# Second half of the output projection: the heads' rests of tiles 1 to 3 placed ahead of tile 1's main products, and tile 2 summed in a bank of its own

## The chip, the core and the metric

The kernel runs on one core of one Trainium2 chip. The metric is the time of one execution on the device in microseconds. Before the change it is 1380.24 us, the median of three runs (1379.95 to 1380.58).

## What is computed

Two decoder layers over 512 tokens of width 1024. Each layer mixes the tokens (layer 0 by a gated convolution, layer 1 by an mLSTM), attends with four heads to a memory of 256 tokens, projects the heads' outputs to width 1024 and adds the layer's input; a layer norm follows, then a mixture of 32 experts, of which a router picks two for each token, and another layer norm.

```python
for i in range(DEPTH):                                    # DEPTH = 2
    h_loc, q_mem = conv_mixer(...) if i % 2 == 0 else mlstm_mixer(...)
    h_mem = cross_attention(q_mem, mem, w_kv_mem[i])
    y = jnp.concatenate([h_loc, h_mem], axis=-1) @ w_out[i]       # 512 x 1024 x 1024
    x = layer_norm(ALPHA * x + y, ln1_g[i], ln1_b[i])
    m = grouped_moe(x, router_w, router_b, w_gate[i], w_up[i], w_down[i])
    x = layer_norm(ALPHA * x + m, ln2_g[i], ln2_b[i])

# in grouped_moe: scores = sigmoid(x2 @ router_w); the best group of 4 experts by the sum of
# its two best; the two best experts in it; gates = their scores, divided by their sum;
# then for each expert: (silu(x @ w_gate[e]) * (x @ w_up[e])) @ w_down[e], times the gate
```

The change touches the line with `w_out` and what is interleaved with it: the sum, the first layer norm and the router.

## The kernel before

**The projection.** The tokens are four tiles of 128 (`TT` = 4), the inner dimension eight slices of 128 (`KT` = 8), the outer dimension two halves of 512 columns. Precision is kept by splitting each operand into a high part and a rest (`hi`, `lo`), so that a slice of a tile takes three products: hi x hi, heads' rest x hi ("the rests"), and hi x weights' rest. The first half of all four tiles is computed slice by slice in banks 0 to 3. The second half follows tile by tile: tile 0 whole (`second(0, ...)`), tile 1 whole (`second(1, ...)`), and for tiles 2 and 3 first the eight products with the heads' rests (`rests(t)`) and later the sixteen others (`mains(t, ...)`: with `w_hi` and `w_lo`). Tile t's second half is summed in `second_bank(t)`, which is bank 4, 5, 4, 3 for tiles 0 to 3; tile 2 therefore waits in `rests(2)` until VectorE has read tile 0's sum out of bank 4 (`summed`).

**What is woven in.** TensorE executes in the order in which `out_pe` is written. Between the products stand, for each tile: `turn(t, b)`, four transposes of half b of the summed rows (for b = 1 they wait for VectorE's sum, `summed`); `route_strips(t)` and `route_sum(t)` (tile 3: `route(3, b)`), the router's logits; `count(t)`, which counts how many earlier tokens picked each expert and waits for VectorE's choice (`chosen`); and `pick_first(t, h)`, which gathers the rows of the first two experts by products.

**VectorE** (`out_dve`) goes tile after tile: `finish_sum(t)` (waits for `b_done`, tile t's last product; adds to the residual at L991, then statistics), `place(t - 1)` (waits for `counted`, L1048 to L1051), `shift`, `invert`, `scale` (layer norm, L1002 to L1010; the last makes `normed`), `scale_logits(t)` (waits for the logits, L1018), `choose(t)` (waits for ScalarE's sigmoid, L1030 to L1042). ScalarE copies the transposes and the strips out of the banks and takes square roots and sigmoids, with a table load between the two.

**The weight stream.** The experts' weights come in units of 2 MB (96 in each layer), in a ring of ten places, all on SyncE's queue and in its order. During the projection the places still hold the projection's own operands, so `out_sp` waits: units 4 and 5 for the first half's end, unit 6 for `rests_read` 1 (the heads' rests are read for the last time, in `rests(3)`), unit 7 for `rests_read` 2 (the weights' rest is read for the last time, in `mains(3, ..., (w_lo,))`), units 8 and 9 for all of the projection (`b_done` 4). Between them SyncE sends each finished tile's rows to memory, after `normed`. From unit 10 on, a load waits until TensorE has read what was in its place; the first three of these units come in pieces, each as soon as a part of the place is free (`part_read`).

```python
second_bank = lambda t: bank[3] if t == TT - 1 else bank[4 + t % 2]
# out_sp
for t in range(TT - 1):
    if t:
        sp.wait_ge(rests_read, t)
        load_unit(sp, l, 5 + t)
    sp.wait_ge(normed, t + 1)
    sp.dma_start(x1_dram[l]..., x_sb[:, t, :]).then_inc(stored, 16)
sp.wait_ge(b_done, TT)
```

The experts themselves (`gate_up`, L1313, and `down`, L1358) run in the order of the stream after it. The whole happens twice, in layer 0 (projection at about 140 to 203 us) and in layer 1 (862 to 921 us).

Of the kernel before, what the change touches and what calls it, by code (L numbers as in the profile page):

```python
# [34 lines left out]
TT = SEQ // P  # L35
KT = D_MODEL // P
# [37 lines left out]
def build_trunk(nc, x, xT_in, memT_in, conv_slabs, conv_qm, mlstm_w_in, smalls, w_kv_mem, w_out,  # L74
                ln1_g, ln1_b, ln2_g, ln2_b, w_pack, out):
    ctx = ExitStack()
    with ctx:
# [56 lines left out]
        bank = [ctx.enter_context(nc.psum_tensor(f"bank{i}", [P, 512], F32)) for i in range(8)]  # L134
# [555 lines left out]
        def out_blocks(l, ph, mem_l, pad, ln_rows, conv, xgT0, ln2_rows, xturned, xcopied, stored, indexed):  # L690
# [20 lines left out]
            in_ln, a_done, b_done, half_summed, summed = s("in_ln"), s("a"), s("b"), s("half_summed"), s("summed")  # L711
# [6 lines left out]
            CODES, PICKED, POS_AT = 2 + PER_GROUP, N_EXPERTS + N_GROUPS, 256  # L718
            w_raw, w_half = w_out_raw, w_out_half
            h_half = heads_half[l]  # L720
            second_bank = lambda t: bank[3] if t == TT - 1 else bank[4 + t % 2]
            logits_of = lambda t: bank[t % 2][:, 0:N_EXPERTS]
            strips_of = lambda t: bank[t % 2][:, P:2 * P]
            pos_of = lambda t: bank[t % 2][:, POS_AT:POS_AT + PICKED]
# [41 lines left out]
            def out_pe(pe):  # L766
                first_ks = range(KT if conv else 6)

                def project(o, n, t, k, first=False):
                    (w_hi, w_lo), (h_hi, h_lo) = ((a[:, k, :] for a in w_half[n]), (a[:, k, t * P:(t + 1) * P] for a in h_half))  # L770
                    for i, (a, b) in enumerate(((h_hi, w_hi), (h_lo, w_hi), (h_hi, w_lo))):
                        if first and i == 0:
                            continue
                        last = nc.tensor.matmul(o[:, :], a, b, start=(k == 0 and i == 0), stop=(k == (KT if n else len(first_ks)) - 1 and i == 2))
                    return last

                def rests(t):
                    if t == 2:
                        pe.wait_ge(summed, 1)
                    else:  # L780
                        pe.wait_ge(half_summed, t + 1)
                    for k in range(KT):
                        last = nc.tensor.matmul(second_bank(t)[:, :], h_half[1][:, k, t * P:(t + 1) * P], w_half[1][0][:, k, :],
                                                start=(k == 0), stop=False)
                    if t == TT - 1:
                        last.then_inc(rests_read, 1)

                def mains(t, ks, parts):
                    for k in ks:
                        for w in parts:  # L790
                            last = nc.tensor.matmul(second_bank(t)[:, :], h_half[0][:, k, t * P:(t + 1) * P], w[:, k, :],
                                                    start=False, stop=(k == KT - 1 and w is parts[-1] and w_half[1][0] in parts))
                    if ks[-1] == KT - 1:
                        last.then_inc(b_done if w_half[1][0] in parts else rests_read, 1)

                def second(t, ks):
                    for k in ks:
                        if t == 0:
                            pe.wait_ge(lo_ready, n_first + k + 1)
                        last = project(second_bank(t), 1, t, k)  # L800
                    if ks[-1] == KT - 1:
                        last.then_inc(b_done, 1)

                def turn(t, b):
                    if b == 0:
                        pe.wait_ge(half_summed, t + 1)
                    else:
                        pe.wait_ge(summed, t + 1)
                    if t == 0 and b == 0:
                        pe.wait_ge(gw_ready, 2)  # L810
                    if t:
                        pe.wait_ge(copied, 2 * t - 1 + b)
                    for j in range(4):
                        k = 4 * b + j
                        last = nc.tensor.transpose(T_BANK[b][:, j * P:(j + 1) * P], x_sb[:, t, k * P:(k + 1) * P], ident[:, :])
                    last.then_inc(turned, 1)

                def may_route(t, b):
                    pe.wait_ge(copied, 2 * t + b + 1)
                    if b == 0 and t < 2:  # L820
                        pe.wait_ge(half_summed, t + 1)
                    elif b == 0:
                        pe.wait_ge(first_marked, 2 * t - 2)

                def route_strips(t):

                    for b in range(2):
                        may_route(t, b)
                        for j in range(4):
                            last = nc.tensor.matmul(strips_of(t)[32 * j:32 * j + 32, :], gw[:, 0, 4 * b + j, :],  # L830
                                                    turned_x[t % 2][:, 4 * b + j, :], start=(b == 0), stop=(b == 1))
                    last.then_inc(routed, 1)

                def route_sum(t):

                    pe.wait_ge(strips_out, t + 1)
                    nc.tensor.matmul(logits_of(t), strips[:, :], strip_sum[:, :], start=True, stop=True).then_inc(routed, 1)
# [9 lines left out]
                def count(t):  # L847

                    pe.wait_ge(chosen, t + 1)
                    for q in range(t + 1):  # L850
                        last = nc.tensor.matmul(pos_of(t), before[:, :] if q == t else ones_bf[:, :],
                                                taken[:, q, :], start=(q == 0), stop=(q == t))
                    last.then_inc(counted, 1)
# [19 lines left out]
                second(0, range(0, 4))  # L873
                turn(0, 0)
                second(0, range(4, KT))
                second(1, range(0, 2))
                turn(0, 1)
                turn(1, 0)
                second(1, range(2, 4))
                route_strips(0)  # L880
                second(1, range(4, 6))
                route_sum(0)
                second(1, range(6, KT))
                rests(2)
                count(0)
                turn(1, 1)
                turn(2, 0)
                rests(3)
                route_strips(1)
                w_hi, w_lo = w_half[1]  # L890
                mains(2, range(0, 2), (w_hi, w_lo))
                route_sum(1)
                mains(2, range(2, KT), (w_hi, w_lo))
                mains(3, range(KT), (w_lo,))
                count(1)
                turn(2, 1)
                turn(3, 0)
                mains(3, range(0, 3), (w_hi,))
                route_strips(2)
                mains(3, range(3, 5), (w_hi,))  # L900
                route_sum(2)
# [83 lines left out]
            def out_dve(dve):  # L985
# [136 lines left out]
                then(V.scalar_tensor_tensor(most[:, 2:3], most[:, 1:2], float(BLK - SLOTS), most[:, 0:1], ALU.add, ALU.max))  # L1122
                then(V.tensor_copy(most_rows[0:1, 0:1], most[0:1, 2:3]))
            return out_sp, out_pe, pick_first, code_rows, out_act, out_dve

        slabs = [(4 * MIX_W, 2 * ML_HEADS + XATT_W)] + [(512 * i, 512) for i in range(6)]
# [16 lines left out]
        def expert_phase(l, mem_l):  # L1143
# [3 lines left out]
            with ph:  # L1147
# [11 lines left out]
                else:  # L1159
# [34 lines left out]
                    l, ph, x1_rows, to_rows, ln_g, ln_b, scattered, acc_read)  # L1194

                out_sp, out_pe, pick_first, code_rows, out_act, out_dve = out_blocks(
                    l, ph, mem_l, pad, ln_rows, conv, xgT[0], (ln_g, ln_b), xturned, xcopied, stored, indexed)
                with nc.Block() as block:
# [1417 lines left out]
```

## Time and profile before

| | us |
|---|---|
| median of the timed runs | 1380.24 |
| the profiled execution, its own time | 1378.45 |
| its span, first to last instruction | 1376.6 |
| TensorE busy in it | 1318.7 (96%) |
| VectorE busy | 507.8 (37%) |
| ScalarE busy | 303.6 (22%) |

The page's slices show the DMA engines moving 427 GB/s through both expert stages and TensorE busy in nearly all of the span; the granted TensorE clock is full in all slices but the last. Of the chain that ended last, the page gives 22% of the span to TensorE and 10% to the DMA of expert weights (`ring<-in_w_pack`). How to read it: a share of busy time doesn't tell which of the two sets the end of a stage; for that one looks at who waits for whom, and when. Spans are us from the start of the profiled execution.

### The profile page before, as it was taken

How to read it: one execution, taken by the hardware profiler on the slowest of the kernel's cores; microseconds unless marked ns; L12 is line 12 of the kernel's file. 1: busy time of each engine (PE TensorE's matmuls, PEld its weight loads, DVE VectorE, ACT ScalarE, POOL GpSimd, SP SyncE). 2: the span in 40 equal slices, each digit the busy share in tenths (PEclk: the TensorE clock that was granted, in tenths of full speed). 3: DMA queues.
4: the chain of work that ended last, by engine and by line, in shares of the span. 5: the costliest groups of instructions: out<-in, count | busy, mean ns of one | idle time of the engine just before them, and what ended most of it. 6: DMA issues, size and time to landing. Idle time of an engine off the chain costs nothing. (4 is left out here: it accounts for less than half of the span.)

```text
span 1376.6 us, 16388 instructions
## 1 busy us (share of the span) xinstructions
PE 1318.7 (96%) x6660; PEld 700.2 (51%) x6660; DVE 507.8 (37%) x1020; ACT 303.6 (22%) x542; POOL 50.6 (4%) x85
## 2 busy tenths in 40 slices
PE   9999999999999989989999999999999999999895
PEld 7878774333333333334787788764333333333331
DVE  6366683133122121222654457772213123122122
ACT  5142341011011010111453236440011011011011
POOL 2000001000000000001000000001000000000000
PEclk9999999999999999999999999999999999999998
DMA  9420989999999999999431201999999999999995
GB/s 372 183 92 0 365 321 422 429 426 426 427 427 427 427 427 428 428 428 383 193 123 62 108 16 70 407 373 426 427 427 427 426 427 428 427 426 428 427 428 210
DMA packets 42548, 465.37 MB, mean 338 GB/s; under 512 B 6730, under 2 KB 7138, under 8 KB 14566
## 3 DMA queue, kind: packets, MB, share of 16 engines
q1 hardware_dynamic: 37574, 454.83, 79.0%
q0 software_dynamic: 4608, 8.40, 1.6%
q8 instruction: 55, 0.90, 0.3%
q10 hardware_dynamic: 288, 1.05, 0.2%
q14 instruction: 23, 0.19, 0.0%
HBM read 460.05 MB, written 12.60 MB: 343 GB/s over the span
## 5 line engine op out<-in xcount | busy, mean ns | idle before, releaser
L1313 PE MATMUL bank<-ring,kv_sb 128*64 128x512 f32 x960 | 216.0, 596 | 14.5 <-DMA ring<-in_w_pack 13.5
L1358 PE MATMUL bank<-ring,pad 128*64 128x512 f32 x928 | 212.0, 598 | 2.5 <-DVE pad L1559 1.2
L1313 PE MATMUL bank<-ring,onehot 128*64 128x512 f32 x896 | 201.0, 596 | 13.1 <-DMA ring<-in_w_pack 13.1
L1313 PEld LDWEIGHTS bank<-ring,kv_sb 128*64 128x64 f32 x960 | 68.3, 137 | 137.5 <-issue 134.7
L1358 PEld LDWEIGHTS bank<-ring,pad 128*64 128x64 f32 x928 | 62.2, 136 | 143.2 <-issue 133.7
L1313 PEld LDWEIGHTS bank<-ring,onehot 128*64 128x64 f32 x896 | 64.1, 137 | 128.6 <-issue 128.4
L1468 ACT ACTIVATE pad<-bank 128x256 f32<-128x256 f32 x64 | 24.5, 383 | 438.2 <-PE bank L1313 438.2
L1474 ACT COPY pad<-bank 128x512 f32<-128x512 f32 x64 | 37.4, 585 | 332.1 <-PE bank L1358 332.1
L1549 DVE COPY onehot<-bank 128x512 f32<-128x512 f32 x32 | 22.1, 692 | 234.5 <-PE bank L1299 234.5
L1559 DVE COPY pad<-bank 128x256 f32<-128x256 f32 x64 | 27.1, 423 | 178.9 <-PE bank L1333 178.9
L1549 DVE COPY kv_sb<-bank 128x512 f32<-128x512 f32 x28 | 19.4, 692 | 185.5 <-PE bank L1299 185.5
L1299 PEld LDWEIGHTS bank<-x_sb 128*128 128x128 f32 x480 | 58.1, 191 | 48.2 <-issue 47.1
L1375 PE MATMUL bank<-pad,x_sb 64*128 64x512 f32 x256 | 71.7, 639 | 0.0
L1299 PE MATMUL bank<-x_sb 128*128 128x128 f32 x480 | 69.5, 288 | 0.7 <-DVE onehot L1549 0.7
L523 PE MATMUL bank<-x_half_hi,w_half_hi 128*128 128x512 f32 x136 | 53.3, 392 | 0.0
L523 PE MATMUL bank<-x_half_lo,w_half_hi 128*128 128x512 f32 x136 | 53.0, 389 | 0.0
L523 PE MATMUL bank<-x_half_hi,w_half_lo 128*128 128x512 f32 x136 | 53.0, 389 | 0.0
L2042 PE MATMUL bank<-x_half_hi,w_half_hi 128*128 128x512 f32 x112 | 44.0, 393 | 0.0
L2042 PE MATMUL bank<-x_half_hi,w_half_lo 128*128 128x512 f32 x112 | 43.7, 390 | 0.0
L2042 PE MATMUL bank<-x_half_lo,w_half_hi 128*128 128x512 f32 x112 | 43.6, 390 | 0.0
L2173 DVE TENSOR_TENSOR w_half_lo<-ring,w_half_hi 128x1024 fp32r<-128x1024 f32 x24 | 29.5, 1239 | 36.8 <-ACT w_half_hi L2133 36.8
L1553 DVE TENSOR_TENSOR pad<-pad,bank 128x256 f32<-128x256 f32 x64 | 26.3, 411 | 29.9 <-ACT pad L1468 29.9
(350 smaller groups left out, 1722.1 us busy)
## 6 DMA issues: line engine op xcount, KB each, us to landing
ring<-in_w_pack SPq DMA_DIRECT2D x164, 2048.0 KB, 30.6
xT<-in_w_pack SPq DMA_DIRECT2D x18, 2048.0 KB, 32.9
ring<-in_w_pack SPq DMA_DIRECT2D x14, 1024.0 KB, 42.2
ring<-in_mlstm_w_in SPq DMA_DIRECT2D x6, 2048.0 KB, 7.6
ring<-in_conv_slabs SPq DMA_DIRECT2D x5, 1536.0 KB, 12.3
ring<-in_w_pack SPq DMA_DIRECT2D x12, 512.0 KB, 7.1
ring<-in_w_out SPq DMA_DIRECT2D x1, 4096.0 KB, 12.8
x_rows<-x_sb SPq DMA_DIRECT2D x6, 512.0 KB, 8.0
```

The lines of the kernel that those rows point to most:

```text
L523: last = nc.tensor.matmul(o[:, :], w[:, k, :], xh[:, k, :], start=(k == 0 and w is w_hi and xh is x_hi), stop=(k == KT - 1 and w is w_lo))
L1299: last = nc.tensor.matmul(o[:, c * P:(c + 1) * P], xg[g % 3][:, 512 * h + c * P:512 * h + (c + 1) * P], pick[g % 2][:, 2 * (q % 2):2 * (q ...
L1313: last = nc.tensor.matmul(GU_BANK[e % 2][64 * f:64 * f + 64, :], xgT[e // 2 % 2][:, 4 * h + c, 64 * (e % 2):64 * (e % 2) + 64], gu[:, c, f ...
L1358: last = nc.tensor.matmul(Y_BANK[e % 2][64 * n:64 * n + 64, :], hidT[e % 2][:, c, 64 * f:64 * f + 64], dn[:, f, c, 512 * n:512 * n + 512], ...
L1375: last = nc.tensor.matmul(ACC[n][:, :], gateT[e // 2 % 2][rows, e % 2, :], y[e % 2][rows, :], start=(j == 0), stop=(j == PER_GROUP - 1))
L1468: nc.scalar.activation(hid[e % 2][:, :], GU_BANK[e % 2][:, 0:256], ACT.Silu).then_inc(activated, 1)
L1474: nc.scalar.copy(y[e % 2][:, :], Y_BANK[e % 2][:, :]).then_inc(y_copied, 1)
L1549: V.tensor_copy(xgT[q % 2][:, 4 * h:4 * h + 4, :], o[:, :].rearrange("p (c r) -> p c r", c=4)).then_inc(xcopied, 1)
L1553: V.tensor_tensor(hid[e % 2][:, :], hid[e % 2][:, :], GU_BANK[e % 2][:, 256:512], ALU.mult).then_inc(hid_done, 1)
L1559: V.tensor_copy(hidT[e % 2][:, :, :].rearrange("p c r -> p (c r)"), H_BANK[:, 0:256]).then_inc(hcopied, 1)
L2042: last = nc.tensor.matmul(o[:, :], w[:, k, :], xh[:, k, :], start=(k == 0 and w is hi and xh is x_hi), stop=(k == KT - 1 and w is lo))
L2173: last = V.tensor_tensor(of(lo), part, of(hi), ALU.subtract)
```

## The change

Tile 2 is summed in bank 2, and tile 3 in bank 3 as before; both are free once VectorE has read the first half's sums. `rests(2)` waits for that (`half_summed`) and no longer for tile 0's second sum. The products with the heads' rests of tiles 1, 2 and 3 now all stand ahead of tile 1's main products, eight at a time between the turns and the router of tile 0; tile 1's sixteen others follow in one piece. Tile 2's main products begin ahead of the turn of tile 1. `count(1)` moves behind the turns of tiles 2 and 3 and three products of tile 3.

```diff
-            second_bank = lambda t: bank[3] if t == TT - 1 else bank[4 + t % 2]
+            second_bank = lambda t: bank[(4, 5, 2, 3)[t]]
...
                 def rests(t):
-                    if t == 2:
-                        pe.wait_ge(summed, 1)
-                    else:
-                        pe.wait_ge(half_summed, t + 1)
+                    pe.wait_ge(half_summed, t + 1)
...
                 second(0, range(4, KT))
-                second(1, range(0, 2))
+                rests(1)
                 turn(0, 1)
                 turn(1, 0)
-                second(1, range(2, 4))
+                rests(2)
                 route_strips(0)
-                second(1, range(4, 6))
+                rests(3)
                 route_sum(0)
-                second(1, range(6, KT))
-                rests(2)
+                w_hi, w_lo = w_half[1]
+                mains(1, range(KT), (w_hi, w_lo))
                 count(0)
+                mains(2, range(0, 2), (w_hi, w_lo))
                 turn(1, 1)
                 turn(2, 0)
-                rests(3)
+                mains(2, range(2, 5), (w_hi, w_lo))
                 route_strips(1)
-                w_hi, w_lo = w_half[1]
-                mains(2, range(0, 2), (w_hi, w_lo))
+                mains(2, range(5, 7), (w_hi, w_lo))
                 route_sum(1)
-                mains(2, range(2, KT), (w_hi, w_lo))
+                mains(2, range(7, KT), (w_hi, w_lo))
                 mains(3, range(KT), (w_lo,))
-                count(1)
                 turn(2, 1)
                 turn(3, 0)
                 mains(3, range(0, 3), (w_hi,))
+                count(1)
                 route_strips(2)
```

TensorE before, from the last products of tile 1 (L774) on: L783 are `rests`, L851 is `count`, L815 are turns, L830 is `route_strips`.

```order
L774 MATMUL bank<-w_out_half_hi,heads_half_lo 128x512
L774 MATMUL bank<-w_out_half_lo,heads_half_hi 128x512
L783 MATMUL bank<-w_out_half_hi,heads_half_lo 128x512 x8
L851 MATMUL bank<-taken,before 128x40
L815 MATMUL bank<-ident,x_sb 128x128 x8
L783 MATMUL bank<-w_out_half_hi,heads_half_lo 128x512 x8
L830 MATMUL bank<-pad,gw 32x128 x8
```

TensorE now, from the end of tile 0 on (lines stand three lower, so L780 are `rests`, L812 turns, L827 and L834 the router of tile 0, L788 are `mains`).

```order
L774 MATMUL bank<-w_out_half_lo,heads_half_hi 128x512
L780 MATMUL bank<-w_out_half_hi,heads_half_lo 128x512 x8
L812 MATMUL bank<-ident,x_sb 128x128 x8
L780 MATMUL bank<-w_out_half_hi,heads_half_lo 128x512 x8
L827 MATMUL bank<-pad,gw 32x128 x8
L780 MATMUL bank<-w_out_half_hi,heads_half_lo 128x512 x8
L834 MATMUL bank<-strip_sum,strips 128x32
L788 MATMUL bank<-w_out_half_hi,heads_half_hi 128x512
L788 MATMUL bank<-w_out_half_lo,heads_half_hi 128x512
```

The last product of tile 1 stood ahead of all 16 rests of tiles 2 and 3; now all 24 rests stand ahead of the first main product of tile 1.

TensorE before, at the end of tile 3's products with `w_lo`: the count of tile 1 (L851), turns, then three products of tile 3 and the router of tile 2.

```order
L791 MATMUL bank<-w_out_half_lo,heads_half_hi 128x512 x9
L851 MATMUL bank<-taken,ones_bf 128x40
L851 MATMUL bank<-taken,before 128x40
L815 MATMUL bank<-ident,x_sb 128x128 x8
L791 MATMUL bank<-w_out_half_hi,heads_half_hi 128x512 x3
L830 MATMUL bank<-pad,gw 32x128 x8
```

The same place now, with the count at L848.

```order
L788 MATMUL bank<-w_out_half_lo,heads_half_hi 128x512 x9
L812 MATMUL bank<-ident,x_sb 128x128 x8
L788 MATMUL bank<-w_out_half_hi,heads_half_hi 128x512 x3
L848 MATMUL bank<-taken,ones_bf 128x40
L848 MATMUL bank<-taken,before 128x40
L827 MATMUL bank<-pad,gw 32x128 x8
```

The count moved behind the eight transposes and three products.

## Rows read from the trace of the kernel before

**Rows 1.** TensorE's waits for weights, total, times, longest: layer 0, then layer 1.
```profile
PE bank L1313 <- DMA ring<-in_w_pack: 12.8, 12, 2.3
...
PE bank L1313 <- DMA ring<-in_w_pack: 13.7, 13, 1.7
```

**Rows 2.** Timeline of TensorE, layer 0's experts: start, duration, [idle before]; the first wait.
```profile
482.96 3.65 PE L1313 MATMUL bank<-ring,kv_sb 128*64 128x512 f32 x16 [0.38 <-DMA ring<-in_w_pack]
```

**Rows 3.** Busy time by stretch; the last three columns: granted clock, DMA share, GB/s.
```profile
177.00:180.00 3.00, 2.83 (x18) 2.25 (x17) 2.77 (x10) 0.86 (x4) 0.00 (x0) 1.00 0.00 0
...
189.00:192.00 3.00, 3.00 (x34) 2.24 (x32) 2.66 (x4) 2.51 (x5) 0.00 (x0) 1.00 1.02 429
...
897.00:900.00 3.00, 3.00 (x31) 2.23 (x29) 2.90 (x8) 1.27 (x3) 0.00 (x0) 1.00 0.50 206
```

**Rows 4.** Timeline of SyncE's queue, layer 0, then layer 1: start, time spent issuing.
```profile
173.97 0.33 SPq L745 DMA_DIRECT2D x_rows<-x_sb  x1
181.72 0.33 SPq L180 DMA_DIRECT2D ring<-in_w_pack  x1
182.75 0.33 SPq L745 DMA_DIRECT2D x_rows<-x_sb  x1
188.20 0.33 SPq L180 DMA_DIRECT2D ring<-in_w_pack  x1
191.56 0.33 SPq L745 DMA_DIRECT2D x_rows<-x_sb  x1
192.92 0.33 SPq L180 DMA_DIRECT2D ring<-in_w_pack  x1
...
203.88 12.16 SPq L186 DMA_DIRECT2D ring<-in_w_pack  x9
...
909.45 0.33 SPq L745 DMA_DIRECT2D x_rows<-x_sb  x1
...
922.12 12.16 SPq L186 DMA_DIRECT2D ring<-in_w_pack  x9
```

**Rows 5.** Issue to landing (last number), issues at 163.2, 173.97, 203.88, 231, 922.12.
```profile
ring<-in_w_pack SPq DMA_DIRECT2D x1, 2048.0 KB, 7.6
...
x_rows<-x_sb SPq DMA_DIRECT2D x1, 512.0 KB, 3.6
...
ring<-in_w_pack SPq DMA_DIRECT2D x1, 512.0 KB, 6.6
...
ring<-in_w_pack SPq DMA_DIRECT2D x1, 2048.0 KB, 10.1
...
ring<-in_w_pack SPq DMA_DIRECT2D x1, 512.0 KB, 6.3
```

**Rows 6.** Timeline of TensorE in layer 0's projection.
```profile
176.55 2.00 PE L783 MATMUL bank<-w_out_half_hi,heads_half_lo 128*128 128x512 f32 x8
...
185.97 2.20 PE L791 MATMUL bank<-w_out_half_lo,heads_half_hi 128*128 128x512 f32 x9
188.01 0.19 PE L851 MATMUL bank<-taken,ones_bf 128*128 128x40 bf16 x1
...
188.90 0.94 PE L791 MATMUL bank<-w_out_half_hi,heads_half_hi 128*128 128x512 f32 x3
```

**Rows 7.** Timeline of VectorE in layer 0's projection.
```profile
175.28 0.25 DVE L1018 SCALAR_TENSOR_TENSOR logit<-bank,mv,shares 128x32 f32<-128x32 f32 x1 [1.34 <-PE bank L837]
...
178.01 0.68 DVE L991 SCALAR_TENSOR_TENSOR x_sb<-x_sb,bank 128x512 f32<-128x512 f32 x1
...
183.57 0.25 DVE L1018 SCALAR_TENSOR_TENSOR logit<-bank,mv,shares 128x32 f32<-128x32 f32 x1 [0.84 <-PE bank L837]
...
186.40 0.69 DVE L991 SCALAR_TENSOR_TENSOR x_sb<-x_sb,bank 128x512 f32<-128x512 f32 x1
...
188.27 0.19 DVE L1048 SCALAR_TENSOR_TENSOR pos<-bank,taken 128x32 f32<-128x32 f32 x1 [0.21 <-PE bank L851]
...
192.32 0.23 DVE L1030 TENSOR_TENSOR sel<-score,smalls_sb 128x64 f32<-128x64 f32 x1 [0.63 <-ACT score L946]
```

## The prediction

> **What bounds the kernel now.** I read four views, in this order. First the chain of waits and TensorE's own waits, to see what the two long expert stages end on. The reader is to see that TensorE waits for nothing but weights there, 12.8 us in layer 0 and 13.7 us in layer 1 [rows 1], and that the first of them comes at 482.96 us [rows 2], some 280 us into the stage of layer 0: until then TensorE works off the ten units of weights that lie ready, and from then on the weight stream sets the time. So the end of each expert stage is the end of its stream, and TensorE may start some microseconds late at no cost (its 12.8 and 13.7 us of waits shrink), as long as the stream itself isn't held up.
>
> Second, the stretches around the change, for the DMA share. The stream stands still at 177 to 180 us and partly at 897 to 900, and from 189 us on it moves 429 GB/s without a break [rows 3]. What the change does to the time is therefore what it does to the idle time of the DMA engines between the sixth and the eleventh unit, about 176 to 210 us and 898 to 928 us.
>
> Third, SyncE's issues and how long they take to land. Unit 6 goes out at 181.72 (it waits for tile 3's rests), the second row store at 182.75, unit 7 at 188.20, the third store at 191.56, units 8 and 9 from 192.92, the first piece of unit 10 at 203.88, when TensorE has read a quarter of unit 0; layer 1 has its third store at 909.45 and its first piece at 922.12 [rows 4]. Alone, a unit lands 7.6 us and a 512 KB store 3.6 us after its issue; the first piece needs 6.6 us though it has the same 512 KB, 6.3 in layer 1, so about 3 us of it are a queue in front of it; the worst of the later units needs 10.1 us [rows 5]. These margins (3.0, 2.7 in layer 1, and 10.1 - 7.6 = 2.5 us) say how late TensorE may free its units before the stream has a hole.
>
> Fourth, TensorE, VectorE in the projection itself: the chain there is VectorE's (sum, layer norm, logits, choice, tile after tile), with TensorE's products fed in between.
>
> **The change part by part.** Products: none is added or removed; 24 products with the heads' rests and 16 main ones stand before tile 1's bank is complete where 24 stood. A product of 512 columns takes (188.01 - 185.97) / 9 = 0.227 us [rows 6].
>
> Tile 1. Its last product began 0.23 us before 176.55 and ended, at 0.39 us for one, at 176.7. Sixteen more before it: 16 x 0.227 = 3.6 us, so 180.3, and VectorE starts its sum 0.1 us later, 180.4. Before it started at 178.01 [rows 7], straight behind tile 0's choice and without waiting. The logits of tile 0 come later too: 24 products stand before them where 18 stood, 6 x 0.227 = 1.36 us; VectorE waits 1.34 us there now [rows 7], and all of the 1.36 is added, so that choice ends at 179.4 and VectorE then stands still for another 1.0 us. Tile 1's sum: 2.4 us late.
>
> Tile 2. Turns of tile 1 wait for this sum, as before, so they are 2.4 us late. Between them and tile 1's logits stand 10 products instead of 12, which gives back 0.45 us: these logits move from 183.57 by +1.95 to 185.5, the 0.84 us of waiting there [rows 7] shrinking to some 0.4, as the layer norm before them is 2.4 late. Tile 2's sum, which no longer waits for its bank, was at 186.40 behind the choice and not behind TensorE, and moves with it to 188.35. Its bank of its own therefore saves nothing that VectorE sees; what it permits is the early rests.
>
> Count of tile 1. TensorE reaches the turn of tile 2 at 187.7 and now waits for tile 2's sum, 188.35 + 0.69 = 189.05: 1.4 us of new standstill, with main products of tile 3 queued behind it. Eight transposes take it to 189.9 (from 188.08 to 188.90 before [rows 6]), three products to 190.7, and only then comes the count, which stood at 188.01. VectorE has its position 0.26 us later, as now (188.01 to 188.27 [rows 6, 7]): 190.95, 2.7 us later than 188.27, of which some 1.0 us is VectorE standing with nothing else to do. Tile 2's layer norm and its row store (191.56 before) move by 2.7 us to 194.25. At tile 2's choice VectorE waits 0.63 us for ScalarE now [rows 7]; that wait was set by the strips' copy and a table load, which move by only 1.1 us, so 0.3 to 0.4 us of the delay is swallowed there. From there on nothing in the chain changes: tile 3's choice, count, first pick, and with them the first expert's products come d = 2.3 us later, and the first piece of unit 10 goes out at 206.2. Bounds for d: if every VectorE wait stays, 2.4 + 2.7 = 5.1; if the whole 0.63 + 0.84 us of waits absorbs it, 2.7 - 1.5 = 1.2. I take 2.3, since each of its steps is a count of products against one row.
>
> The stream. Unit 6: rests of tile 3 now end at about 176.4 instead of 181.6, and SyncE, which has issued the first row store at about 174.4 (0.4 later), sends it at 176.6, 5.1 us sooner, into the standstill. It is in by 184. That is a gain only if the rest follows. The second store goes out 2.4 us late (185.1), unit 7 depends on the low parts of w for tile 3, at 187.9 (0.3 sooner), and lands at 195.4. The third store, 194.25, is the gate: units 8 and 9 stand behind it in SyncE's order. Their own condition, tile 3's last product, is met at about 193.9. So between 195.4 and 194.25 + 3.6 = 197.85 little lands. From there the rest is bandwidth: units 8 and 9, the fourth store and the first piece are 5.24 MB, 12.2 us at 429 GB/s [rows 3], so the first piece lands at 210.1. Before, it landed at 203.88 + 6.6 = 210.5 [rows 4, 5]. Its own issue sets no later time, 206.2 + 3.6 = 209.8. The stream is 0.4 us ahead. Later the worst unit would want 2.3 + 7.6 = 9.9 us against the 10.1 it had [rows 5], less the 0.4 gained: the stream keeps 0.2 to 0.4 us. In layer 1 the order and the gaps are the same; there the third store goes 2.7 us late from 909.45 to 912.15, so the first piece lands at 912.15 + 3.6 + 12.2 = 927.95, against 922.12 + 6.3 = 928.4 [rows 4, 5]: the same 0.4, with the smaller margin, so again about 0.3.
>
> The row shows 3.6 us for a 0.52 MB store, 2.4 us of it beyond the 1.22 that its bytes take at 429 GB/s [rows 3, 5]. The Trainium skill (DMA: Bandwidth & Descriptors, "Anatomy of one DMA — SWDGE (gpsimd) path") gives a DMA a fixed cost of about 2.0 us beside its bytes at 436 GB/s, fitted on GpSimd's path, which speaks against each issue into an empty queue, and this change adds two of those. By that rule, an estimate, the store costs 3.2 us, the piece lands 0.4 us sooner, and the stream would be 0.8 ahead; nothing in the sum hangs on it, since the margin of the later units caps the gain.
>
> Sum: -0.35 x 2 = -0.7 us. The profiled execution took 1378.45 us (span 1376.6 and 1.85 around it), so 1377.75 for its like; the median of the timed runs lies 1.79 above it, so 1379.5. I forecast 1379.6, no change that can be told.
>
> **Rivals.** (a) Slower: TensorE's delay outgrows the stream's margin. One mechanism: the late count of tile 1 and the late bank of tile 1 hold VectorE's chain, the first piece goes out late, and each microsecond of d beyond about 2.7 is a hole in the stream, in each layer. At d = 4 that is 2 x 1.3 = 2.6 us, 1382.9; at the bound 5.1, 2 x 2.4 = 4.8 us, 1385.1. For it: the margins are 2.5 to 3.0 us, hardly more than d, and the gathers on GpSimd's queue share the bandwidth. Against: each wait was counted with its neighbours. It decides from d = 2.7 us on.
>
> (b) Faster: VectorE's chain isn't held up, because the products run or are released sooner than I count. Then units 8 and 9 go out as before at 192.9 into an engine that has already moved unit 6, and the piece lands at its own limit, 203.88 + 3.6 = 207.5: 3.0 us a layer, 1374.3. For it: unit 6 does go 5 us sooner, and the stream stands still for it. Against: sixteen products more before tile 1's bank are 3.6 us, and there were only 1.3 us between its end and its reading. In between (d near 1) some 2 us a layer would remain, 1376.
>
> (c) The change does nothing to the stream, because unit 6 was never late for the stream's end: then only d counts, and as it stays under the margin the time is 1380.2. It can't be told from the forecast by its time.
>
> **How the numbers follow.** Forecast with (c): 0.68, its own range 1378.0 to 1382.5. (a): 0.20, of which most lies under 1383.5. (b): 0.12. The range that should hold it 8 times in 10 is 1377.0 to 1383.5. Less than 0.2% (2.8 us) can't be told from no change here; so faster 0.12, same 0.68, slower 0.20.
>
> **What would show it.** In the profile after: VectorE's tile 1 sum at about 180.4 behind a wait for TensorE; TensorE idle for 1.4 us before tile 2's turn; VectorE waiting some 1 us for the count of tile 1; unit 6 issued at 176.6 and the third store at 194.3; the first piece of unit 10 issued at 206.2 instead of 203.88; TensorE's total wait for weights 2 to 3 us shorter in each expert stage, with the same stage end. I'm wrong if the first piece lands after 211.5 or before 209, or if DMA share falls visibly under 1.0 between 215 and 240 us.

## The result and the profile after

The changed kernel takes 1382.61 us (median of 16 runs, 1381.13 to 1383.59), the kernel before, in the runs beside it, 1379.57 us (16 runs, 1378.42 to 1381.15). The ratio is 1.0020, with a 95% interval of 1.0013 to 1.0027: 2.8 us slower, 1.8 to 3.7. The forecast was 1379.6 us and no change. The profiled execution took 1381.13 us, span 1379.3. All ratios, here and below, are of fast executions; one execution of 1692.6 us at a granted clock of 0.75, of the kernel with twelve dummy products, is left out of them.

VectorE in layer 0's projection, timeline of the changed kernel (start, duration, [idle before <- releaser]; source lines stand three lower than before):

```profile
176.55 0.25 DVE L1015 SCALAR_TENSOR_TENSOR logit<-bank,mv,shares 128x32 f32<-128x32 f32 x1 [2.25 <-PE bank L834]
...
180.31 0.69 DVE L988 SCALAR_TENSOR_TENSOR x_sb<-x_sb,bank 128x512 f32<-128x512 f32 x1 [0.94 <-PE bank L788]
...
185.47 0.25 DVE L1015 SCALAR_TENSOR_TENSOR logit<-bank,mv,shares 128x32 f32<-128x32 f32 x1 [0.44 <-PE bank L834]
...
188.25 0.68 DVE L988 SCALAR_TENSOR_TENSOR x_sb<-x_sb,bank 128x512 f32<-128x512 f32 x1
...
190.88 0.19 DVE L1045 SCALAR_TENSOR_TENSOR pos<-bank,taken 128x32 f32<-128x32 f32 x1 [0.97 <-PE bank L848]
...
194.52 0.23 DVE L1027 TENSOR_TENSOR sel<-score,smalls_sb 128x64 f32<-128x64 f32 x1 [0.30 <-ACT score L943]
```

Each of these answers to one of [rows 7]: 180.31 was forecast as 180.4, 185.47 as 185.5, 188.25 as 188.35, 190.88 as 190.95. The chain is held up as worked out, by TensorE's products ahead of tile 1's sum and by the count of tile 1. TensorE, the same stretch:

```profile
188.99 1.09 PE L812 MATMUL bank<-ident,x_sb 128*128 128x128 f32 x8 [1.19 <-DVE x_sb L988]
```

It stands still for 1.2 us ahead of tile 2's turn (forecast 1.4). SyncE's queue, to be read against [rows 4]:

```profile
174.33 0.33 SPq L745 DMA_DIRECT2D x_rows<-x_sb  x1
176.41 0.33 SPq L180 DMA_DIRECT2D ring<-in_w_pack  x1
185.05 0.33 SPq L745 DMA_DIRECT2D x_rows<-x_sb  x1
187.83 0.33 SPq L180 DMA_DIRECT2D ring<-in_w_pack  x1
194.09 0.33 SPq L745 DMA_DIRECT2D x_rows<-x_sb  x1
194.46 0.43 SPq L180 DMA_DIRECT2D ring<-in_w_pack  x1
...
205.94 12.16 SPq L186 DMA_DIRECT2D ring<-in_w_pack  x9
```

Unit 6 goes out 5.3 us sooner, the third store 2.5 us later, the first piece of unit 10 2.06 us later (203.88 to 205.94, d = 2.06 where 2.3 was forecast). Layer 1 repeats it: its first piece goes out at 925.47 instead of 922.12, of which 1.2 us come with the later end of layer 0, so 2.1 us are its own. Up to here all is as predicted. Unit 9, the last one ahead of the first piece (issued at 194.93; its place is called `xT`), lands at 207.8; the prediction's working gives 207.6. The landing of the first piece is not as predicted (DMA issues by line, issues at 194.93 and 205.94, last number from issue to landing; compare [rows 5]):

```profile
xT<-in_w_pack SPq DMA_DIRECT2D x1, 2048.0 KB, 12.9
...
ring<-in_w_pack SPq DMA_DIRECT2D x1, 512.0 KB, 5.6
```

The first piece lands at 211.5, 1.0 us later than before and not 0.4 sooner, and 3.7 us behind unit 9 where the prediction has 2.4; before, the same piece landed 1.6 us behind unit 9 (issued at 193.29, landed 15.6 us later). The stretches show where the stream lost it. Before (the last two columns are DMA share and GB/s):

```profile
204.00:207.00 3.00, 3.00 (x18) 1.45 (x16) 3.00 (x5) 0.32 (x1) 0.00 (x0) 1.00 0.91 389
207.00:210.00 3.00, 3.00 (x16) 1.00 (x14) 0.61 (x1) 1.55 (x2) 0.00 (x0) 1.00 1.02 416
210.00:213.00 3.00, 3.00 (x48) 1.52 (x46) 0.80 (x5) 0.38 (x1) 0.00 (x0) 1.00 1.03 414
213.00:216.00 3.00, 3.00 (x18) 1.00 (x16) 2.66 (x12) 0.00 (x0) 2.24 (x2) 1.00 1.03 421
```

and after:

```profile
204.00:207.00 3.00, 2.54 (x14) 0.93 (x14) 3.00 (x5) 0.65 (x2) 0.00 (x0) 1.00 0.96 407
207.00:210.00 3.00, 3.00 (x20) 1.48 (x18) 2.67 (x5) 1.24 (x2) 0.00 (x0) 1.00 0.85 258
210.00:213.00 3.00, 3.00 (x16) 0.83 (x12) 0.00 (x0) 0.63 (x1) 0.00 (x0) 1.00 0.99 336
213.00:216.00 3.00, 3.00 (x48) 1.74 (x48) 1.64 (x9) 0.39 (x1) 0.46 (x1) 1.00 1.03 410
```

In these 12 us (389 + 416 + 414 + 421) x 3 = 4.92 MB moved before and 4.23 MB after. The 0.69 MB that are missing are 1.6 us of a stream of 429 GB/s. Note the third row: a DMA share of 0.99 at 336 GB/s. The engines count as busy, and the stream is a fifth slow all the same.

Ahead of these 12 us little is lost. Longer stretches, before:

```profile
174.00:192.00 18.00, 17.83 (x122) 14.03 (x120) 13.95 (x37) 10.16 (x17) 0.00 (x0) 1.00 0.63 233
192.00:204.00 12.00, 10.66 (x86) 9.11 (x87) 10.79 (x35) 4.70 (x10) 0.00 (x0) 1.00 1.03 421
```

and after:

```profile
174.00:192.00 18.00, 16.81 (x124) 12.80 (x114) 12.02 (x35) 9.57 (x18) 0.00 (x0) 1.00 0.67 245
192.00:204.00 12.00, 10.11 (x88) 9.46 (x87) 10.92 (x35) 5.06 (x8) 0.00 (x0) 1.00 0.98 392
```

In us of 429 GB/s, the stream is 12 x 18 / 429 = 0.5 ahead at 192 us, thanks to the early unit 6; it loses 29 x 12 / 429 = 0.8 around the late third store, and is 0.3 behind at 204. The 1.6 us of the hand-over come on top.

For all kernels below I use one stretch, 158 to 240 us, to put a number on the lag of the stream in layer 0: 82 us x (GB/s of before - GB/s of the kernel) / 429. Both ends lie in full flow, so a start that differs by some tenths cancels. Before:

```profile
158.00:240.00 82.00, 79.54 (x527) 50.99 (x525) 47.64 (x122) 20.71 (x37) 5.81 (x5) 1.00 0.93 376
```

After:

```profile
158.00:240.00 82.00, 77.50 (x517) 50.27 (x517) 47.61 (x122) 20.75 (x37) 5.82 (x5) 1.00 0.92 365
```

The lag is 82 x 11 / 429 = 2.1 us (one GB/s is 0.2 us; the megabytes of the same stretch, 30.82 and 29.95, give 2.0). It stays: from 158 to 640 us, nearly the end of the stream, 201.53 MB moved before and 200.68 after, again 2.0 us. TensorE's waits for weights, layer 0 and layer 1, against 12.8 and 13.7 in [rows 1]:

```profile
PE bank L1310 <- DMA ring<-in_w_pack: 12.0, 12, 1.2
...
PE bank L1310 <- DMA ring<-in_w_pack: 12.9, 13, 1.2
```

They shrank by 0.8 us, not by the 2.1 that TensorE is late: the stream has moved along with it, and the stage ends later. The last piece of layer 0's stream and TensorE's last product with it, before (issued at 600.30, landed at 642.2; the product ends at 646.07):

```profile
ring<-in_w_pack SPq DMA_DIRECT2D x1, 1024.0 KB, 41.9
...
644.08 1.99 PE L1375 MATMUL bank<-pad,x_sb 64*128 64x512 f32 x8
```

and after (issued at 602.48, landed at 643.5; the product ends at 647.36):

```profile
ring<-in_w_pack SPq DMA_DIRECT2D x1, 1024.0 KB, 41.0
...
645.37 1.99 PE L1372 MATMUL bank<-pad,x_sb 64*128 64x512 f32 x8
```

The last piece lands 1.3 us later and the stage ends 1.3 us later. Two layers with 1.3 to 1.4 us each are the 2.8 us that were measured; twice the lag would be 4.0, more than the interval allows. The landings of single units behind unit 12 are between 0.4 and 2.1 us late (unit 13: 231.7 and 233.7), though the bytes are 2.0 late all the time. A unit has landed when the last of its bytes has; why the last piece is only 1.3 late isn't settled.

### The profile page after: what moved, and what is told of

Same layout as the page of the kernel before. It is cut to its first block and busy times, and to the rows that moved or that the text cites. A ratio compares the mean times of both kernels' runs of the same rounds, so it can differ in the third digit from the quotient of the medians.

```text
span 1379.3 us, 16387 instructions
## 1 busy us (share of the span) xinstructions
PE 1318.3 (96%) x6659; PEld 699.7 (51%) x6660; DVE 507.6 (37%) x1020; ACT 304.4 (22%) x542; POOL 50.7 (4%) x85
## 5 line engine op out<-in xcount | busy, mean ns | idle before, releaser
L1310 PE MATMUL bank<-ring,kv_sb 128*64 128x512 f32 x960 | 216.0, 596 | 13.7 <-DMA ring<-in_w_pack 12.6
## 6 DMA issues: line engine op xcount, KB each, us to landing
ring<-in_w_out SPq DMA_DIRECT2D x1, 4096.0 KB, 12.8
```

The costliest lines, as they stand in the source:

```text
L1310: last = nc.tensor.matmul(GU_BANK[e % 2][64 * f:64 * f + 64, :], xgT[e // 2 % 2][:, 4 * h + c, 64 * (e % 2):64 * (e % 2) + 64], gu[:, c, f ...
```

## The experiments

The hand-over is the point at 204 us where the units that found a free place end and those begin for which TensorE must free it. Two theories at the start. H, hand-over: the queue in front of the first pieces covers only about 1 us of delay, and what goes beyond it is lost in each layer. M: the margin of the prediction (2.7 us) holds, and the loss comes from elsewhere, for instance from the standstills that the early unit 6 leaves. Times are given as ratios to the kernel before on the same chip (95% interval in brackets), and in us of its 1379.8 (1379.5 for the last two kernels).

### Delay alone: 1, 2 and 4 us in the kernel before

```diff
                 pick_first(pe, 2, 1)
                 pick_first(pe, TT - 1, 0)
+                for _ in range(7):        # 12, 21
+                    nc.tensor.matmul(bank[3][:, :], ones_bf[:, :], zero_bf[:, :].broadcast_to([P, 512]), start=True, stop=True)
```

> The kernel before with seven small dummy products (1.5 us, 0.46 of it in an existing wait) right ahead of the first expert's products in each layer: the first pieces go out about 1.05 us late, nothing else moves. H: within the cover, 0 to +0.8 us in all. M: 0.

> The same with twelve dummy products: the first pieces go out about 2.1 us late, which is the delay of the changed kernel, without its other edits. H: +1 to +1.8 us a layer, so +2 to +3.6 us, with a stretch of low GB/s behind unit 9. M: 0 to +0.5 us.

> The same with twenty-one dummy products: the first pieces go out about 4.1 us late. H: +3 to +3.8 us a layer, so +6 to +7.6 us. M: (4.1 - 2.7) x 2 = +2.8 us.

Measured: 1.0002 (0.9993 to 1.0010), +0.3 us; 1.0016 (1.0008 to 1.0025), +2.2 us; 1.0033 (1.0020 to 1.0046), +4.6 us. The lags of the stream in layer 0, from the rows of the three kernels, in this order:

```profile
158.00:240.00 82.00, 79.96 (x528) 51.44 (x529) 47.66 (x122) 20.73 (x37) 5.82 (x5) 1.00 0.93 374
```

```profile
158.00:240.00 82.00, 79.95 (x528) 51.62 (x529) 47.64 (x122) 20.73 (x37) 5.82 (x5) 1.00 0.93 369
```

```profile
158.00:240.00 82.00, 79.95 (x528) 51.76 (x527) 46.29 (x119) 20.71 (x37) 5.81 (x5) 1.00 0.91 358
```

They are 0.4, 1.3 and 3.4 us for first pieces 1.0, 2.1 and 4.0 us late. M wanted 0, 0 and 1.4. So the cover is some 0.6 to 0.7 us (the lags by megabytes in the table at the end, 0.3, 1.4 and 3.5, agree), a quarter of what I had, and beyond it each microsecond goes through to the stream. In the times the slope is weaker than twice the lag (4.6 us, with an interval of 2.8 to 6.3 from five runs, for 6.9): H had 6 to 7.6 and M 2.8, and this time alone decides for neither; the lags and the +2.2 us of the second kernel, where M had at most 0.5, do. The profiled execution of the four-microsecond kernel was 7.0 us longer than that of before, which was itself 1.3 us under its median; what of this is more than scatter stays open.

In the four-microsecond kernel next to nothing stands in front of the first piece: between 208.5 and 209 us the DMA engines are busy for 6% of the time, with the ends of unit 9 (landed at 209.8) and of the fourth row store. The landings of its first and third piece, issued at 208.20 and 209.92 us:

```profile
ring<-in_w_pack SPq DMA_DIRECT2D x1, 512.0 KB, 4.4
...
ring<-in_w_pack SPq DMA_DIRECT2D x1, 512.0 KB, 6.6
```

and its stretches:

```profile
207.00:210.00 3.00, 3.00 (x14) 0.97 (x14) 0.88 (x1) 0.00 (x0) 0.00 (x0) 1.00 0.73 239
210.00:213.00 3.00, 3.00 (x18) 1.54 (x19) 0.00 (x0) 1.87 (x2) 0.00 (x0) 1.00 0.85 254
213.00:216.00 3.00, 3.00 (x38) 1.24 (x35) 0.00 (x0) 0.38 (x1) 0.00 (x0) 1.00 0.99 298
216.00:219.00 3.00, 3.00 (x30) 1.25 (x29) 2.30 (x11) 0.00 (x0) 1.20 (x1) 1.00 1.00 397
```

A piece that goes out nearly alone takes 4.4 us, not 3.6, and the third one, with only two pieces ahead of it, takes 6.6, as long as the first piece of the kernel before. By the subtraction of the prediction, 6.6 - 4.4 = 2.2 us would be the queue in front; the measured cover is 0.6 to 0.7. So the time from issue to landing doesn't give the cover, not even with the right figure for a lone piece. And the stream needs some 9 us to come back to its rate. The 3.6 us for the lone store weren't a lone store's either: at 173.97 the last unit of the first six was still landing (the stretch from 174 to 177 us moves 265 GB/s). The changed kernel has a store that goes out into an empty queue, at 185.05:

```profile
x_rows<-x_sb SPq DMA_DIRECT2D x1, 512.0 KB, 2.6
```

Bytes to move aren't what is missing behind the gap: when the fourth piece goes out, at 212.01, 1.57 MB have been issued and 0.65 moved on this queue, and at 213.73 it is 2.62 and 1.21. But these are only two or three pieces at a time. That the rate is held down by their small number, each of them taking over 4 us, is a rival to a slow restart as such, and no run sets the two apart.

### The count back in its place

```diff
                 mains(3, range(KT), (w_lo,))
+                count(1)
                 turn(2, 1)
                 turn(3, 0)
                 mains(3, range(0, 3), (w_hi,))
-                count(1)
```

> The changed kernel with count(1) back in its old place, ahead of tile 2's turn. TensorE stands still there anyway (1.2 us), so the count costs nothing, and VectorE's wait of 0.97 us before tile 2's layer norm goes. The first piece of unit 10 should be issued about 1 us sooner than in the changed kernel, some 1.1 us later than in the kernel before. Theory H (hand-over: the queue in front of the first pieces covers only about 1 us of delay, and what goes beyond is lost in each layer): about 2 us faster than the changed kernel, 0 to 1 us slower than before (1379.6 to 1380.6). Theory M (the 2.7 us margin of the prediction holds, and the loss comes from elsewhere, for instance from the idle DMA stretches at 183 to 185 and 187 to 188 us that the early unit 6 leaves): as slow as the changed kernel, 3 us over before.

Measured: 1.0013 (1.0005 to 1.0022), +1.8 us, about 1.0 less than the changed kernel, with intervals that overlap, and more than the 0 to 1 that H gave. The first piece goes out 1.0 us late, as expected. VectorE reads the count without waiting for it:

```profile
190.37 0.15 DVE L1045 SCALAR_TENSOR_TENSOR pos<-bank,taken 128x32 f32<-128x32 f32 x1
```

and the stream lags by 82 x 4 / 429 = 0.8 us instead of 2.1:

```profile
158.00:240.00 82.00, 78.72 (x521) 50.90 (x521) 47.47 (x122) 20.71 (x37) 5.81 (x5) 1.00 0.93 372
```

The moved count is thus more than half of the lag in the trace; the times alone don't show it. What is left when it is back is by elimination tile 1's late sum, which still makes the third store 1.5 us late.

### Tile 2's bank alone

```diff
-            second_bank = lambda t: bank[3] if t == TT - 1 else bank[4 + t % 2]
+            second_bank = lambda t: bank[(4, 5, 2, 3)[t]]
...
-                    if t == 2:
-                        pe.wait_ge(summed, 1)
-                    else:
-                        pe.wait_ge(half_summed, t + 1)
+                    pe.wait_ge(half_summed, t + 1)
```

> The kernel before with tile 2's second half in bank 2, and its rests waiting for the first half's sums only; the order of all products as before. Both theories: nothing waited for bank 4, so the time of before, 1379.8 us within 0.5.

Measured: 0.9999 (0.9990 to 1.0008). The bank is worth nothing and costs nothing (within 1.4 us), and the stream moves 375 GB/s in the stretch where it moved 376. The loss sits in the order of the products.

### Unit 6 held back in the changed kernel

```diff
                     if t:
+                        if t == 1:
+                            sp.wait_ge(summed, 2)
                         sp.wait_ge(rests_read, t)
                         load_unit(sp, l, 5 + t)
```

> The changed kernel with SyncE's issue of unit 6 held back until VectorE's second sum of tile 1, so that it goes out at about 181 us instead of 176.4, nearly when it went out before. H (what counts is how late the first pieces are and what is queued in front of them): the early unit 6 is worth nothing, since the queue runs dry again behind it; the time of the changed kernel, 1382.6 us within 0.5. Rival E (the early unit 6 leaves the idle stretches that cost the time): 1 to 3 us faster than the changed kernel. Rival G (the early unit 6 is a gain that the rest of the change eats up): 1 to 3 us slower than the changed kernel.

Measured: 1.0022 (1.0012 to 1.0032), +3.0 us, not to be told from the changed kernel. E falls: the early unit 6 isn't what costs the time. G can't be told either; in the trace the lag is 82 x 13 / 429 = 2.5 us against 2.1, so the 4.6 us by which this kernel sends unit 6 later cost about 0.4 us a layer, which fits the 0.5 us that the changed kernel was ahead at 192 us. The lag's last digit is 0.2 us, and the time can't show so little. The profiled execution was the slowest of the nine.

```profile
158.00:240.00 82.00, 77.50 (x516) 51.15 (x516) 46.63 (x120) 20.71 (x37) 5.81 (x5) 1.00 0.92 363
```

### The third store and units 8 and 9 late, alone and with the delay

```diff
                     sp.wait_ge(normed, t + 1)
+                    if t == 2:
+                        sp.wait_ge(turned, 2 * TT)
                     sp.dma_start(x1_dram[l]...
```

(the second of the two kernels has the twelve dummy products as well)

> The kernel before with SyncE's third row store, and units 8 and 9 behind it, held until tile 3's last turn, at about 194.3 us, as late as in the changed kernel (store 2.7 us, units 1.5 us late); TensorE and VectorE as before, so the first pieces are on time. H: the queue in front of units 8 and 9 had about 2 us, so the stream is 0 to 0.5 us late when the first pieces come, and that passes through: 0 to +1 us in all.

> Both delays together on the kernel before: the third store and units 8 and 9 held to 194.3 us, and twelve dummy products (2.1 us) ahead of the first expert. H: this is all that the changed kernel does to the stream, so its time, about +3 us; more than the +2 us of twelve dummy products alone. If the order of the products costs something beyond the stream, the changed kernel is slower than this one.

Measured: 1.0018 (1.0009 to 1.0027), +2.5 us, for the late store and units alone, and 1.0023 (1.0014 to 1.0033), +3.2 us, for both. Nearly as much as the whole change comes from holding SyncE's issues though TensorE and VectorE are as before: more than I had expected. Both kernels hold the issues back a little more than the change does: counted from SyncE's first issue in the projection, the third store is 2.9 us late and unit 8 1.9, against 2.6 and 1.6 in the changed kernel. The kernel with the late store and units alone, where its queue had nearly run dry (unit 7 lands at 196.8):

```profile
195.00:198.00 3.00, 2.85 (x28) 2.75 (x27) 2.70 (x12) 2.08 (x4) 0.00 (x0) 1.00 0.96 336
198.00:201.00 3.00, 2.27 (x24) 2.08 (x23) 2.72 (x12) 0.21 (x1) 0.00 (x0) 1.00 0.97 347
```

Before, in the same stretches:

```profile
195.00:198.00 3.00, 2.85 (x28) 2.75 (x27) 2.70 (x13) 1.73 (x4) 0.00 (x0) 1.00 1.02 421
198.00:201.00 3.00, 2.27 (x23) 2.08 (x23) 2.76 (x10) 0.00 (x0) 0.00 (x0) 1.00 0.99 421
```

((421 - 336) + (421 - 347)) x 3 / 429 = 1.1 us are lost in six microseconds in which the engines were busy for 96% of the time. Over the layer the lag is 82 x 8 / 429 = 1.5 us:

```profile
158.00:240.00 82.00, 79.54 (x526) 51.34 (x526) 47.66 (x122) 20.71 (x37) 5.81 (x5) 1.00 0.92 368
```

With both delays it is 1.9 us, not 1.5 + 1.3:

```profile
158.00:240.00 82.00, 79.95 (x527) 51.42 (x528) 47.66 (x122) 20.71 (x37) 5.81 (x5) 1.00 0.92 366
```

The two overlap: a stream that is late already finds the late first pieces in time. Together they give the time of the changed kernel (+3.2 against +2.8 us, each within about a microsecond) and its lag (1.9 against 2.1). So late issues and late first pieces are enough to explain the change. Since either alone already gives most of it, the runs don't say how the 2.8 us divide between them.

### Larger first pieces

```diff
-FIRST_PIECES = (tuple((a, a + 1024) for a in range(0, 4096, 1024)), ((0, 1024), (1024, 2048), (2048, 4096)),
-                ((0, 2048), (2048, 4096)))
+FIRST_PIECES = (((0, 2048), (2048, 4096)),) * 3
```

> The changed kernel with units 10 to 12 loaded in six pieces of 1 MB (8 KB a row) instead of six of 512 KB and three of 1 MB: the first piece goes out one step of TensorE, 0.9 us, later, so the hand-over has a longer gap. H1 (the stream restarts slowly because its packets are small): behind the gap the stream is back at over 400 GB/s within 2 us instead of 5, and the time is the changed kernel's or up to 1.5 us less. H2 (what counts is only how late the first piece is): 0.9 us more a layer, 1.5 to 2 us slower than the changed kernel.

> The same pieces in the kernel before: the first goes out 0.9 us later into a queue that still has some 3 us of work. H1: 0 to 0.5 us faster than before, since the stream runs at 429 instead of some 415 GB/s there. H2: 0 to +1 us (in the dummy-product kernels 1.05 us of delay cost 0.3 us in all).

Measured: in the changed kernel 1.0019 (1.0010 to 1.0028), +2.6 us; in the kernel before 0.9995 (0.9986 to 1.0004), -0.7 us, unclear. H2 falls: its time would be 4.3 us or more over before. Its execution starts 0.7 us later than that of the changed kernel; counted from SyncE's first issue, the first piece goes out 0.9 us later, as expected, and the stream's lag isn't larger, 82 x 10 / 429 = 1.9 us:

```profile
158.00:240.00 82.00, 77.49 (x516) 50.57 (x516) 47.55 (x122) 20.73 (x37) 5.81 (x5) 1.00 0.92 366
```

But H2 was put to a weak test: the first large piece goes out just when the second small one did (206.80 after this shift), so only the first 512 KB are late. H1's return to over 400 GB/s within 2 us doesn't come. In the 12 us behind its own first piece this kernel moves as much as the changed one. The larger pieces, then the changed kernel:

```profile
207.49:219.49 12.00, 12.00 (x90) 4.91 (x88) 6.92 (x23) 2.25 (x3) 2.67 (x3) 1.00 0.96 357
```

```profile
205.94:217.94 12.00, 12.00 (x90) 4.91 (x88) 7.07 (x22) 2.25 (x3) 2.10 (x2) 1.00 0.97 355
```

So nothing here shows that the packets' size is what makes the return slow. In the kernel before the stream moves 377 instead of 376 GB/s in the common stretch, no more than one step of the row.

**All kernels side by side.** Microseconds late against the kernel before, in layer 0, each counted from SyncE's first issue in the projection (139.46 in the kernel before). The lag is worked out from the megabytes from 158 to 240 us. The end is that of TensorE's last product for layer 0's experts.

| kernel | third store | first piece | lag of the stream | end of the experts | time |
|---|---|---|---|---|---|
| changed | 2.6 | 2.2 | 2.0 | 1.4 | +2.8 |
| 7 dummy products | 0 | 1.0 | 0.3 | 0.2 | +0.3 |
| 12 dummy products | 0 | 2.1 | 1.4 | 0.7 | +2.2 |
| 21 dummy products | 0 | 4.0 | 3.5 | 3.1 | +4.6 |
| count back | 1.5 | 1.0 | 0.8 | 1.2 | +1.8 |
| bank alone | 0 | 0 | 0.1 | 0.2 | 0 |
| unit 6 held | 2.6 | 2.2 | 2.4 | 3.7 | +3.0 |
| store, units 8, 9 late | 2.9 | 0 | 1.6 | 1.3 | +2.5 |
| both delays | 2.9 | 2.1 | 1.8 | 1.9 | +3.2 |
| changed, large pieces | 2.6 | 3.0 | 1.8 | 1.7 | +2.6 |
| before, large pieces | 0 | 0.9 | -0.2 | -0.2 | -0.7 |

The time covers two layers and many executions, the other columns one layer of one execution, and that of unit 6 held was the slowest of its kernel. In every kernel the last piece of the stream lands late by the same figure as the end of the experts, within 0.03 us: the stage ends with its stream. That figure is up to 0.7 us below the lag of the bytes and, in the kernel with unit 6 held, 1.3 above it, so the lag tells where a delay comes from better than what it costs.

## Why the prediction was wrong

**What bounds the kernel: right.** The kernel with late store and units shows it best: TensorE and the first pieces are on time, only the stream is held, and it takes 2.5 us longer. In every kernel the stage in layer 0 ends as late as its last piece lands. "From 189 us on it moves 429 GB/s without a break" was too good, though: the stretches of the kernel before go from 389 to 437, and at the hand-over, 204 to 207 us, they stand at 389 with a DMA share of 0.91. The hand-over had hardly anything to spare already.

**The change part by part, to the first piece: right.** The times of VectorE's chain and SyncE's issues came within 0.3 us, d as 2.06 against 2.3. That the bank saves nothing was right too (0.9999).

**The margins: wrong, and this is the step that failed.** "Alone, a unit lands 7.6 us and a 512 KB store 3.6 us after its issue; the first piece needs 6.6 us though it has the same 512 KB [...] so about 3 us of it are a queue in front of it". The store wasn't alone (alone it takes 2.6 us), the piece is a load and not a store, and a load nearly alone takes 4.4. Even 6.6 - 4.4 = 2.2 us isn't the margin. The measured cover is 0.6 to 0.7 us where I had 2.7, and d = 2.06 lies far beyond it.

**"From there the rest is bandwidth": wrong.** This is the same error seen in the stream. The working holds to the landing of unit 9 (207.6 for 207.8). For what follows I let the stream run at 429 GB/s, and took "Its own issue sets no later time" from the 3.6 us of the store. It ran at 258 and 336 GB/s for 6 us, and the piece landed at 211.5 instead of 210.1. At the third store the stream lost 0.8 us, which the early unit 6 paid for up to 0.5; at the hand-over it lost 1.6.

**The term of the sum.** I had the stream 0.35 us ahead in each layer. It was 2.0 us behind in layer 0 and the stage ended 1.3 later. The sum's sign (-0.7) rested on a margin read off latencies.

**The rival that came true is (a)**, with its mechanism as described and its threshold wrong: it decides from about 0.7 us on, not from 2.7. It leaves out the late third store, which alone cost +2.5 us. Its formula with the measured cover, (2.06 - 0.65) x 2 = 2.8 us, is the measured 2.8, but that is luck: the trace has a lag of 2.0 a layer and not 1.4, and only the last landing is no more than 1.3 late. The time lay inside the stated range, also by luck, since I gave (a) a chance of 0.20 and forecast no change.

**The other rivals.** (b), faster by an early unit 6: the issue was early, and worth about 0.4 us a layer. (c), no change because d stays under the margin: it fell with the margin. Of the signs, the first piece landed at the very edge that I had set (211.5), the DMA share stayed at 1.0 between 215 and 240 us, and TensorE's waits shrank by 0.8 us a layer instead of 2 to 3.

## What to carry to other kernels

When a stream of weights sets the end, ask at each point where its queue is refilled by a computed event how late that event may come, and measure it with a few dummy products rather than reading it off the time from issue to landing: that time holds a start-up that no queue explains (4.4 us for a piece whose bytes take 1.2 at full rate). Look at the next transfers before moving one forward: here the gain of 5.3 us on one issue was worth about 0.4, since those behind it were gated by the chain that the move delays. A gap in the queue cost the gap and the slow return behind it. And follow the delay to the last landing of the stream, not only to the bytes behind the gap: here the bytes were 2.0 us late, the last landing 1.3.

## What the runs showed of the hardware

A DMA share of 0.96 to 1.03 doesn't mean full rate: behind a dry or nearly dry queue shares of 0.96 to 0.99 went with 298, 336 and 347 GB/s, in the running stream 1.01 to 1.03 with 410 to 430. Loads of 512 KB took 4.4 us nearly alone, a row store of 512 KB 2.6 us alone. Larger pieces (8 KB a row instead of 4 KB) moved as much in the 12 us behind the first one (357 against 355 GB/s). What keeps the rate down for 6 to 9 us isn't settled.
